# The 768-token feed-forward of an fp32 transformer pair: eight block products against seven, chunks of four against chunks of eight

## What is computed

```python
x = x + 0.5 * ml[2] * swiglu_2(modulate(rms_norm(x, norm1_g), ml[0], ml[1]), ffn1_w_in, ffn1_w_out)
cx = cx + 0.5 * mc[2] * swiglu_2(modulate(rms_norm(cx, norm1_g), mc[0], mc[1]), ffn1_w_in, ffn1_w_out)
...
a, b = jnp.split(h @ w_in, 2, axis=-1)
return (jax.nn.silu(a) * b) @ w_out
```

## Time and profile before

| | us |
|---|---|
| median of three executions | 2543.92 (2543.29 to 2544.47) |
| the profiled execution's own time | 2543.39 |
| its span in the trace | 2541.6 |
| `ffn3`, from the norm before it to its last matmul | 1070.6 to 1623.3 |
| `ffn4`, its seven-product units | 2225 to 2494 |
| mean granted TensorE clock | 0.998 |

### The profile page before, as it was taken

The page is one execution under the profiler, slowest core; times in us unless marked ns, Lnnn a source line. Parts: engine busy times, 40 slices in busy tenths (PEclk is TensorE's granted clock), DMA queues, the critical chain, the costliest instruction groups (busy, mean ns, idle before and its releaser), DMA issues.

```text
span 2541.6 us, 34889 instructions
## 1 busy us (share of the span) xinstructions
PE 2502.3 (98%) x12916; PEld 2094.4 (82%) x12916; DVE 1452.5 (57%) x2236; ACT 815.9 (32%) x1224; POOL 385.7 (15%) x311
## 2 busy tenths in 40 slices
PE   8999999989999999999999999999999999999998
PEld 7888888765788888888888888888888768899997
DVE  7677656789476433453444334444226754667684
ACT  4112233368432222411111112222322552344443
POOL 2101023020120111311011002103001104211112
PEclk9999999999999999999999999999999999999999
DMA  6444435420344332333322331223332013232332
GB/s 200 147 135 149 141 107 133 102 70 18 99 125 140 95 98 85 104 100 100 100 89 87 97 100 58 76 90 100 94 102 77 25 51 95 71 116 84 117 88 78
DMA packets 372354, 250.63 MB, mean 99 GB/s; under 512 B 22864, under 2 KB 368528, under 8 KB 372240
## 3 DMA queue, kind: packets, MB, share of 16 engines
q1 hardware_dynamic: 372240, 249.10, 32.4%
HBM read 237.73 MB, written 2.10 MB: 94 GB/s over the span
## 4 chain that ended last, share of the span: by engine, by line
PE 90%; DVE 6%; ACT 2%; issue 1%; SPq 0%; DMA 0%; POOL 0%; DVEq 0%; ACTq 0%; POOLq 0%
PE PS L1087 22%; PE PS L1094 21%; PE PS L1089 21%; PE PS L1062 3%; PE PS L1065 3%; PE PS L1063 3%; PE PS L1225 2%; PE PS L1226 2%; PE PS L1227 2%; PE PS L1667 2%; PE PS L1017 1%; PE PS L1659 1%; PE PS L1470 1%; DVE WL L2177 1%; PE PS L1303 1%
## 5 line engine op out<-in xcount | busy, mean ns | idle before, releaser
L1087 PE MATMUL PS<-NH,WH 128*128 128x512 f32 (+1 forms) x1824 | 526.7, 370 | 4.6 <-DVE WL L2177 2.1
L1089 PE MATMUL PS<-NH,WL 128*128 128x512 f32 (+1 forms) x1824 | 524.4, 369 | 0.0
L1094 PE MATMUL PS<-NL,WH 128*128 128x512 f32 (+1 forms) x1824 | 496.2, 369 | 0.0
L1697 ACT ACTIVATE WH<-RAW 128x2048 fp32r<-128x2048 f32 (+1 forms) x166 | 315.6, 1901 | 456.4 <-PE PS L1094 447.4
L2177 DVE TENSOR_TENSOR WL<-RAW,WH 128x2048 fp32r<-128x2048 f32 (+1 forms) x166 | 397.6, 2395 | 86.4 <-ACT WH L1697 85.6
L1094 PEld LDWEIGHTS PS<-NL,WH 128*128 128x128 f32 x1824 | 331.1, 189 | 60.1 <-POOL NL L3030 0.7
L1087 PEld LDWEIGHTS PS<-NH,WH 128*128 128x128 f32 x1824 | 327.9, 188 | 63.5 <-issue 5.9
L1089 PEld LDWEIGHTS PS<-NH,WL 128*128 128x128 f32 x1824 | 330.6, 188 | 59.5
L2988 POOL CAST HH<-VA 128x512 f32 (+2 forms) x88 | 71.6, 814 | 1264.1 <-DVE VA L2339 996.6
L1087 PE MATMUL PS<-HH,WH 128*128 128x512 f32 (+1 forms) x820 | 235.5, 369 | 0.0
L1089 PE MATMUL PS<-HH,WL 128*128 128x512 f32 (+1 forms) x820 | 235.1, 368 | 0.0
(11 more groups left out here) (404 smaller groups left out, 3711.0 us busy)
## 6 DMA issues: line engine op xcount, KB each, us to landing
RAW<-in_ffn_w_in SPq DMA_DIRECT2D x88, 512.0 KB, 4.6
MW<-in_w_mod SPq DMA_DIRECT2D x72, 512.0 KB, 3.4
RAW<-in_w_in SPq DMA_DIRECT2D x70, 512.0 KB, 4.0
RAW<-in_w_gate SPq DMA_DIRECT2D x44, 512.0 KB, 3.7
RAW<-in_w_up SPq DMA_DIRECT2D x44, 512.0 KB, 4.8
RAW<-in_w_down SPq DMA_DIRECT2D x32, 512.0 KB, 4.2
RAW<-in_ffn_w_out SPq DMA_DIRECT2D x32, 512.0 KB, 4.1
RAW<-in_w_out SPq DMA_DIRECT2D x16, 512.0 KB, 3.8
```

The lines of the kernel that those rows point to most:

```text
L1087: pe.matmul(outs[half][x], w[half][0], xh(k), start=i == 0, stop=False)
L1089: pe.matmul(outs[half][x], w[half][1], xh(k), start=False, stop=False)
L1094: last = pe.matmul(outs[half][x], w[half][0], xl(k), start=False, stop=i == kn - 1)
L1697: act.activation(WH[1 - s][:, 0:cols], RAW[1 - s][:, 0:cols], ACT.Copy).then_inc(w_hi, 1)
```

## The change

`ffn3` gets the scheme of `ffn4`, with halves of 384 tokens (768 in two), and chunks `CHUNKS3 = (4, 4, 4, 4, 4, 2)`. The first chunk's four gate-and-up units stay plain; the 18 others become seven-product units of 84 matmuls of 384 columns. There are now six groups of four down units, 24 in all. The activations' block sums are made by DVE once (`half_sum3`: ten operations on 128x1536, in the plain units 1 to 3 and in the first down unit), with four high parts on ACT and four low parts on DVE (`half_low3`), in the space that HL, MW and CXIN leave; hidden tiles have buffers for four. The 30 modulation tiles lie in the four plain units, in the last chunk's two gate-and-up units and in all 24 down units, and are summed in RB in place of CXIN. Sums of weight blocks go to spare slots of WHF and WLF and, in place, to RAW. ACT and DVE split only the used columns of a down unit (1024, in the last chunk 512 on DVE). `run_ahead` takes two low parts between its sums, in `ffn4` too. The number of down matmuls is the same.

```diff
+CHUNKS3 = (4, 4, 4, 4, 4, 2)
...
+        T12H = sb("T12H", [P, 2, KD // 2, (T + TC) // 2], F32R, f3)
...
-        PAIR0 = {0: 0, 8: 4, 12: 6, 20: 10, 24: 12, 30: 15, 38: 19, 42: BOTH, 50: BOTH + 4, 54: BOTH + 6, 62: BOTH + 10,
-                 66: BOTH + 12}
+        PAIR0 = {0: 0, 8: 4, 12: 6, 20: 10, 24: 12, 30: 15, 38: 19}
+        PAIR0.update({m: BOTH + (m - M0["ffn3"]) // 2 for m in range(M0["ffn3"], 2 * MOD_PAIRS, 2)})
+        MOD_CHUNKS = [ffn3[0][0], ffn3[-1][0]]
...
-            return CXIN[:, 1:2, :] if m0 >= M0["ffn3"] else VA[:, :, T:T + TC]
+            return MACC[:, 1:2, :] if m0 >= M0["ffn3"] else VA[:, :, T:T + TC]
...
-            return CXIN[:, 0:1, :] if m0 >= M0["ffn3"] else MACC
+            return MACC[:, 0:1, :] if m0 >= M0["ffn3"] else MACC
...
+        def still_mods(m0, j):
+
+            return m0 if m0 is not None and m0 + j < 2 * MOD_PAIRS else None
...
+        SV3 = Seven(ffn3, CHUNKS3, T + TC, 0)
+        SV4 = Seven(ffn4, CHUNKS, T, SV3.u1)
...
+        def sum_to(b, n):
+
+            if sv_of(b) is SV4:
+                return SM[:, n, :]
+            spare = slice(3 * T, 4 * T)
+            return (WHF[1 - SV3.s0][:, spare], WLF[1 - SV3.s0][:, spare],
+                    quarter(RAW, b % 2, 1, 0), quarter(RAW, b % 2, 0, 1))[n]
...
+        def st_parts(b):
+
+            h = sv_of(b).half
+            p = [SF[:, n * h:(n + 1) * h] for n in range(2 * (T + TC) // h)]
+            if sv_of(b) is SV4:
+                return p
+            first = p[3 * (unit(b) % 2)]
+            return first, p[1], p[2], first, p[1], p[2]
...
-            ffn(ffn3, w1, 0, w1, DFF, inp["ffn1_w_out_2"][0], name="ffn3")
+            k0, m0 = 0, M0["ffn3"]
+            for kn, (bg, bd) in zip(CHUNKS3, ffn3):
+                with_mods = bg in MOD_CHUNKS
+                gate_up(bg, kn, w1, k0 * P, w1, DFF + k0 * P, m0 if with_mods else None, True)
+                m0 += kn if with_mods else 0
+                pairs(bd, KD // 2, inp["ffn1_w_out_2"][0], k0, kn, 0, True, m0)
+                k0, m0 = k0 + kn, m0 + KD // 2
...
+            def ffn_sevens(sv, m, h0, xs, hs, banks):
+                for c, (kn, (bg, bd)) in enumerate(zip(sv.chunks, sv.stages)):
+                    b0 = bg
+                    if c == 0:
+                        gate_up(bg, PLAIN, xs, banks, None, m=m, straight=True)
+                        b0 += PLAIN
+                    if b0 in RUNS:
+                        seven_products(b0, *RUNS[b0])
+                    pairs(bd, KD // 2, hs, banks, kn, (h_split, h0), True)
...
+            def half_high(sv, i):
+
+                act.wait_ge(t_sum, (T_SUM4 if sv is SV4 else T_SUM3)[i])
+                if sv is SV4:
+                    n = {3: 0, 2: 1, 4: 2, 6: 3}[i]
+                    h, f = TH[:, n, :, :], TF[:, n, :, :]
+                elif i in (2, 3):
+                    h, f = T12H[:, 3 - i, :, :], T12F[:, 3 - i, :, :]
+                elif i == 4:
+                    h, f = T3H[:, :, :], T3F[:, :, :]
+                else:
+                    h, f = (z[:, 0:KD // 2, sv.half:sv.tok] for z in (NH, NLF))
+                act.activation(h, f, ACT.Copy).then_inc(t_hi, 1)
...
-                if u:
+                if sv is SV3 and n == 3:
+                    dve.wait_ge(st_lo, 6 * u + 2)
+                elif u and not (sv is SV3 and n == 2):
                     dve.wait_ge(st_lo, 6 * (u - 1) + (4, 3, 5, 6)[n])
+                    if n == 1:
+                        dve.wait_ge(st_sum, 4 * u)
                 a11, a12, a21, a22 = (quarter(RAW, s, r, c) for r in range(2) for c in range(2))
-                x, y, op = ((a21, a22, ALU.add), (SM[:, 0, :], a11, ALU.subtract), (a11, a21, ALU.subtract),
-                            (a12, SM[:, 1, :], ALU.subtract))[n]
-                dve.tensor_tensor(SM[:, n, :], x, y, op).then_inc(st_sum, 1)
+                x, y, op = ((a21, a22, ALU.add), (sum_to(b, 0), a11, ALU.subtract), (a11, a21, ALU.subtract),
+                            (a12, sum_to(b, 1), ALU.subtract))[n]
+                dve.tensor_tensor(sum_to(b, n), x, y, op).then_inc(st_sum, 1)
 
...
                     wait(dve, psum_free, after(b, 0))
                     dve.wait_ge(st_copy, 3 * u + 1)
                     dve.wait_ge(st_pe, 6 * u + 2)
-                    dve.tensor_tensor(ST_G0, chain(b, 1), ST_P1, ALU.add).then_inc(st_gate, 1)
+                    dve.tensor_tensor(g0, chain(b, 1), p1, ALU.add).then_inc(st_gate, 1)
                     low(0)
-                    if m == 7:
+                    mods(b0, b - b0, b % 2, still_mods(m0, b - b0))
+                    if m == 7 and sv is SV4:
                         factor_sum(b + 1, 2)
                     low(1)
+                    if m == 7 and sv is SV3:
+                        factor_sum(b + 1, 2)
                     if m == 7:
                         factor_sum(b + 1, 3)
                     low(2)
...
+                    mods_out(b0, b - b0, b % 2, still_mods(m0, b - b0))
 
             def run_ahead(b0):
 
-                for n in range(4):
-                    factor_sum(b0, n)
                 for i in range(4):
-                    factor_low(b0, i)
+                    if i < 2:
+                        factor_sum(b0, i)
+                    elif i == 2:
+                        factor_low(b0, 0)
+                        factor_low(b0, 1)
+                        factor_sum(b0, 2)
+                        factor_sum(b0, 3)
+                factor_low(b0, 2)
+                factor_low(b0, 3)
 
             def halves_summed():
 
...
+            def added(to, first, x, op1, more):
+
+                tsum.settle(dve, dve.tensor_tensor(to, first, x, op1))
+                for y, op in more:
+                    tsum.settle(dve, dve.tensor_tensor(to, to, y, op))
+
+            def half_sum3(i):
+
+                if i == 3:
+                    for m in (norm_c1, norm_x1):
+                        dve.wait_ge(norm_hi, m.low + KD)
+                        for k in range(KD):
+                            dve.wait_ge(*low_ready(m, k))
+                    added(T12F[:, 0, :, :], half_of(NH, 0, 1), half_of(NH, 0, 0), ALU.subtract,
+                          ((half_of(NL, 0, 1), ALU.add), (half_of(NL, 0, 0), ALU.subtract)))
+                elif i == 4:
+                    added(T3F[:, :, :], half_of(NH, 1, 1), half_of(NH, 0, 1), ALU.subtract,
+                          ((half_of(NL, 1, 1), ALU.add), (half_of(NL, 0, 1), ALU.subtract)))
+                elif i == 2:
+                    added(T12F[:, 1, :, :], half_of(NH, 1, 1), T12F[:, 0, :, :], ALU.subtract,
+                          ((half_of(NL, 1, 1), ALU.add),))
+                else:
+                    dve.wait_ge(pe_done, ffn3[0][1])
+                    added(NLF[:, 0:KD // 2, SV3.half:SV3.tok], half_of(NH, 1, 0), T12F[:, 1, :, :], ALU.subtract,
+                          ((half_of(NL, 1, 0), ALU.add),))
+
+            def half_low3(i):
...
+            def plain_first3(b0, g0, h0, m0):
+
+                for b in range(b0, b0 + PLAIN):
+                    j, s = b - b0, b % 2
+                    if j:
+                        mods(b0, j, s, m0)
+                    split(s, b, SLOT if j < PLAIN - 1 else CHUNKS3[0] * 2 * P)
+                    if j == 0:
+                        final_applied()
+                        mods(b0, j, s, m0)
+                    else:
+                        half_sum3((3, 4, 2)[j - 1])
+                    if j == PLAIN - 1:
+                        half_low3(3)
+                        half_low3(4)
+                    dve.wait_ge(gate_done, g0 + j + 1)
+                    wait(dve, h_split, after(h0 + j, -1))
+                    dve.tensor_tensor(VA[:, s, T:SV3.tok], SA[:, s, T:SV3.tok], CU[s][:, 0:SV3.tok - T], ALU.mult)
+                    dve.tensor_tensor(VA[:, s, 0:T], SA[:, s, 0:T], U[s][:, :], ALU.mult).then_inc(psum_free, 1)
+                    mods_out(b0, j, s, m0)
 
             def plain_first(b0, g0, h0):
 
...
+            def halves_late(j):
+
+                if j == 0:
+                    half_sum3(6)
+                    half_low3(2)
+                elif j == 1:
+                    half_low3(6)
...
+                    if b0 in RUNS:
+                        seven_products(b0, *RUNS[b0], kn, h0 + b0 - bg, m0 if bg in MOD_CHUNKS else None)
+                    m1 = m0 + kn if bg in MOD_CHUNKS else m0
+                    down(bd, sv.tok, by, by_ctx, True, m1, cols=kn * 2 * P, before=halves_late if sv is SV3 and c == 0 else None)
+                    m0 = None if m1 is None else m1 + KD // 2
                     h0 += kn
...
+                    m0 = still_mods(m, j) if straight else m
                     mods(b0, j, s, m0)
                     if run:
                         run_ahead(b + 1)
                     elif at is not None and not tail:
-                        split(s, b)
+                        split(s, b, cols if not isinstance(j, int) or j < KD // 2 - 1 else SLOT)
```

(28 more changed lines are left out.)

242 lines of the change are left out of this document (140 added, 102 removed).

## The result

The changed kernel takes 2521.5 us (median of 4 runs, 2521.34 to 2521.67) against 2544.19 for the one before (2543.29 to 2544.81): a ratio of 0.9911, with an interval of 0.9894 to 0.9928. The profiled execution took 2521.56 us with a span of 2519.8, where the one before had 2543.39 and 2541.6. So the prediction of 2520 was 1.5 us low, and the direction and the range were right.

The account below looks back on a forecast made before the run. The prediction took PE's own work to bound the kernel. Its terms, -38.4 + 0.5 + 2.2 + 1.1 + 10.1 + 1.0, gave -23.5 against 2543.39, so 2520 us, range 2510 to 2532.

Parts of the forecast that it names:

- 18 seven-product units: ffn3's new gate-and-up units: 84 matmuls at 173.3 ns make 14.56 us against 16.69, -38.4 us in all.
- starts of runs: At five run starts PE loses 0.1 us each to DVE's order, +0.5 us; ends 0 and 6.5.
- first down group: First chunk's down units: DVE's added block sum and low part make PE wait for a split, +2.2 us; ends 0 and 5.
- last chunk, first gate-and-up unit: A modulation tile ahead of the addition on DVE makes it late for PE, +1.1 us; ends 0 and 3.
- last down group: Last chunk's down units: DVE's list outlasts PE's 4.16 us a unit, +10.1 us, 1.5 of it for POOL; ends 8 and 17.
- half clock in the norm: Norm behind ffn3: PE's idle time drops its clock partly to 1.2 GHz, +1.0 us; ends 0 and 2.
- DVE in a new unit: In a seven-product unit of ffn3 DVE is busy 11.1 of 14.56 us, so hidden behind PE.
- rival (c): DVE bounds the new units with a list of 17.7 us, giving 2577 us; chance 0.03.
- Rival (a): Five run starts cost 1.3 us each, four steps from gate to down 1 us each: +10, 2530 us; chance 0.14.
- POOL's share: In the last down group POOL's five additions of squares cost DVE 1.5 us, of 0 to 8.7 possible.

Follow-up runs that it names:

- plain_fours: The changed kernel with ffn3's gate-and-up units computed from plain products again, keeping the six chunks and the new places of the modulation; 2559.86 us.
- combined: mods_early with modulation behind the low parts in seven-product units and two low parts one unit later in the first down group; 2514.93 us.
- no_pool_adds: The changed kernel without POOL's five additions of squares ahead of the norm behind ffn3; 2518.23 us.
- mods_early: The changed kernel with the last down group's four modulation tiles moved to the second chunk's gate-and-up units; 2516.6 us.
- kept_warm: The changed kernel with small unused matmuls on PE before the last down unit's weights and behind the last group; 2522.06 us.
- small_second: The changed kernel with the two-tile chunk second instead of last, its modulation moved with it; 2517.01 us.

## Why the prediction was right

It was right by its mechanism and by its main terms, and the errors of the others are small and partly cancel. Against the sum of the prediction:

```
term                                   predicted   measured
18 seven-product units                   -38.4       -38.3   (14.56 us against 16.69)
starts of runs                            +0.5         0.0
first down group                          +2.2        +1.9   (third unit 10.25 us against 8.35)
last chunk, first gate-and-up unit        +1.1        +0.9   (15.44 us against 14.56)
last down group                          +10.1       +12.2   (30.4 us against 18.2)
half clock in the norm                    +1.0        +1.45  (7.24 us against 5.79)
sum                                      -23.5       -21.9   (stretch -22.06)
```

**PE's work.** The interpolation between 256 and 512 columns held to the second decimal: 173.3 ns a matmul. The 2.5 ns over the columns that the prediction quoted from the Trainium skill (TensorE: Matmul & The Clock Gate, "Wait — 56ns, not 53.3ns?") do not hold here; the rows' 13.3 ns do. `plain_fours` gives 38.29 for the whole term, with the help of the chance named there; the reading that rests on nothing else is 18 x (16.69 - 14.56).

**DVE in a new unit** is busy 11.49 us of 14.56 where the prediction added up 11.1, and outside the last chunk PE waited for it nowhere inside a run, so rival (c) had 3 us to go.

**Starts of runs.** The two units around a start take 14.50 and 8.42 in place of 14.56 and 8.35, their sum unchanged in four of five. I had put 0.1 at each for the row of ffn4; the 2.08 us products leave more room than that. Rival (a) has no row on its side.

**First down group and last chunk's first unit.** Both came where the step said, on WL and on SA, at 0.3 and 0.2 us less than added up. `combined` shows that both are DVE's order and not its load: with the same operations in another order they leave 0.2 and nothing, and 0.7 at the first run's start.

**Last down group.** This is the mis-sized term: some 27 us from the last gate unit to the last addition were forecast, and it is 30.4 to the norm. The sum without POOL was 8.6 and is 7.9 (26.1 - 18.2, from `no_pool_adds`). POOL's share was the step "I take 1.5, nearer the low end", and measured 4.3. It rested on the split of 2048 columns, which was to last 2.28 us with POOL beside it or not the earlier trace rows. The split of that row shows only the one half, since POOL's last additions had ended 1.7 us before it (1616.61). The other half holds in the kernel before too, but its timelines of DVE and POOL show in which order the two start:

```profile
1588.03 2.28 DVE L2177 TENSOR_TENSOR WL<-RAW,WH 128x2048 fp32r<-128x2048 f32 x1
...
1600.74 2.29 DVE L2177 TENSOR_TENSOR WL<-RAW,WH 128x2048 fp32r<-128x2048 f32 x1
```
```profile
1589.38 2.08 POOL L3021 TENSOR_TENSOR VA<-VA,SA 128x512 f32<-128x512 f32 x1 [9.09 <-ACT SA L1718]
1601.38 4.23 POOL L3021 TENSOR_TENSOR VA<-VA,SA 128x512 f32<-128x512 f32 x2 [9.92 <-ACT SA L1718]
```

DVE was first both times, and POOL's additions took 2.08 and 4.23 for what lasts 1.45 and 2.69 in the changed kernel: POOL paid. In `mods_early` POOL was first, by 0.42 us (1592.30 against 1592.72), and the split took 3.02. So a long DVE operation that was under way was safe, and a row of it says nothing of four short ones, which POOL can get in front of at each boundary, as it does at 1581.68. The Trainium skill, SBUF — State Buffer, "Who interferes with whom", says that a DVE instruction with two SBUF inputs contends with a GpSimd one that reads SBUF, and that the order of issue decides which of them is blocked. The order of starting in these rows agrees with it. Had POOL held DVE for all of its time, its additions would have cost the list 8.7 us, and I took 1.5; each addition held up the one short operation that was next, and they cost half of 8.7.

**The clock** fell in the norm as predicted and cost 1.45 us; it fell also in the last down unit, which had not been forecast, for nothing, since DVE's list runs on without a break there (10.26 us to the norm against 10.23 in `kept_warm`).

## What to carry to other kernels

A cut in the matmuls of this stage showed up whole as long as the other engines' lists fitted into the new, shorter unit; where they don't fit, here at the first and the last group of the stage, add up the list of each engine and look also at the ones that only start to overlap because the units got shorter. A row that shows an operation undisturbed beside another engine is evidence only for operations of that length and that order of starting. And the order of the pieces (which chunk is small, what stands ahead of what in a list) was worth 10 us here, nearly half of the change's net gain and a quarter of what the products brought, with not an operation removed.

## What the runs showed of the hardware

Two things were not expected. POOL's work holds up an operation with one tensor input too: TENSOR_SCALAR on 256 columns (its other operand is a scalar for each partition) takes 0.35 us alone (1586.41 in `no_pool_adds`) and 1.98 when POOL's operation on the hidden tile (1573.56, 1.80 us) runs beside it. The two records start 0.02 us apart, too close to say which was first. In DVE's timeline of the changed kernel:

```profile
1573.54 1.98 DVE L2334 TENSOR_SCALAR RB<-MW,CV 128x256 f32<-128x256 f32 x1
```

And a fall of the clock can come in one kernel and not in the next at the same wait. The wait of 1.89 us on POOL at the head of the small group passed without one in the changed kernel, in `no_pool_adds` and in `small_second`, and had one right behind it in `kept_warm`; 3.46 us at the norm had none in `mods_early`, and 3.47 us there had one in `combined` (0.79 granted from 1591 to 1599). So the length of the wait alone does not decide it. What does was not tried.
